# Sums of weights made ahead in DRAM, and 43 units of seven half products in place of 26

## What is computed

```
def sqrelu_mlp(hn, w1, w2):                 # w1 1024 x 4096
    u = jnp.square(jax.nn.relu(hn @ w1))
    return u @ w2

def swiglu(h, w_in, w_out):                 # w_in 1024 x 5632, run twice
    gate, up = jnp.split(h @ w_in, 2, axis=-1)
    return (jax.nn.silu(gate) * up) @ w_out
```

## Time and profile before

| | |
|---|---|
| median of 3 runs | 2059.39 us (2058.56 to 2064.13) |
| the profiled execution | 2055.45 us, its span 2053.5 us |
| PE busy | 1970.8 us (96%) |
| DVE, ACT, POOL busy | 1226.9 us (60%), 806.8 us (39%), 432.2 us (21%) |
| DMA | 175.06 MB, mean 85 GB/s |

### The profile page before, as it was taken

The page is one execution under the profiler, slowest core; times in us unless marked ns, Lnnn a source line. Parts: engine busy times, 40 slices in busy tenths (PEclk is TensorE's granted clock), DMA queues, the critical chain, the costliest instruction groups (busy, mean ns, idle before and its releaser), DMA issues.

```text
span 2053.5 us, 29329 instructions
## 1 busy us (share of the span) xinstructions
PE 1970.8 (96%) x11954; PEld 1717.1 (84%) x11954; DVE 1226.9 (60%) x1633; ACT 806.8 (39%) x1069; POOL 432.2 (21%) x312
## 2 busy tenths in 40 slices
PE   8999989999999999999999999999997899999996
PEld 6788766788888888999899999998884578888895
DVE  6668756656565654122566566556897557566565
ACT  4448734533232433223353232234434444233232
POOL 2012230202113220013222121212245122032122
PEclk9999999999999998999999999999998999999998
DMA  4223111123232221211123233223131022223231
GB/s 176 103 83 115 62 62 62 62 103 103 86 103 100 91 95 42 82 42 42 62 83 103 83 103 104 83 103 103 62 106 40 22 83 102 103 83 103 99 106 62
DMA packets 27850, 175.06 MB, mean 85 GB/s; under 512 B 4409, under 2 KB 4537, under 8 KB 7762
## 3 DMA queue, kind: packets, MB, share of 16 engines
q1 hardware_dynamic: 25680, 167.32, 23.6%
q0 software_dynamic: 1888, 5.90, 0.9%
q10 hardware_dynamic: 162, 0.10, 0.0%
HBM read 171.19 MB, written 4.78 MB: 86 GB/s over the span
## 4 chain that ended last, share of the span: by engine, by line
PE 72%; issue 12%; DVE 6%; POOL 4%; ACT 4%; DMA 2%; SPq 0%; POOLq 0%; DVEq 0%; ACTq 0%
PE lin L533 50%; PE lin L1833 6%; PE aux L1833 5%; POOL squares L752 2%; DMA w_raw<-in_weights 1%; PE aux L1425 1%; ACT w_hi L442 1%; PE aux L2645 1%; PE lin L1627 1%; PE lin L1380 1%; DVE w_lo L449 1%; PE lin L2615 1%; POOL w_lo L449 1%; PE aux L2629 1%; POOL r_t L2245 1%
## 5 line engine op out<-in xcount | busy, mean ns | idle before, releaser
L533 PE MATMUL lin<-x_hi,w_hi 128*128 128x512 f32 (+1 forms) x1160 | 408.8, 352 | 14.5 <-DVE tmp L628 6.5
L533 PE MATMUL lin<-x_hi,w_lo 128*128 128x512 f32 (+1 forms) x1160 | 407.0, 351 | 0.0
L533 PE MATMUL lin<-x_lo,w_hi 128*128 128x512 f32 (+1 forms) x1160 | 406.8, 351 | 0.0
L449 DVE TENSOR_TENSOR w_lo<-w_raw,w_hi 128x2048 fp32r<-128x2048 f32 (+1 forms) x118 | 276.3, 2341 | 176.4 <-ACT w_hi L442 175.6
L533 PE MATMUL lin<-v_hi,w_hi 128*128 128x264 f32 (+1 forms) x1088 | 365.3, 336 | 9.0 <-DVE tmp L1873 4.1
L533 PE MATMUL lin<-v_hi,w_lo 128*128 128x264 f32 (+1 forms) x1088 | 361.3, 332 | 0.0
L533 PE MATMUL lin<-v_lo,w_hi 128*128 128x264 f32 (+1 forms) x1088 | 360.9, 332 | 0.0
L442 ACT ACTIVATE w_hi<-w_raw 128x2048 fp32r<-128x2048 f32 (+1 forms) x129 | 242.8, 1882 | 206.2 <-PE lin L533 196.1
L533 PEld LDWEIGHTS lin<-x_hi,w_hi 128*128 128x128 f32 x1160 | 219.4, 189 | 49.5 <-DVE tmp L628 7.3
L533 PEld LDWEIGHTS lin<-x_hi,w_lo 128*128 128x128 f32 x1160 | 219.7, 189 | 29.9
L533 PEld LDWEIGHTS lin<-x_lo,w_hi 128*128 128x128 f32 x1160 | 219.5, 189 | 30.0 <-issue 0.2
(11 more groups left out here) (449 smaller groups left out, 3937.7 us busy)
## 6 DMA issues: line engine op xcount, KB each, us to landing
w_raw<-in_weights SPq DMA_DIRECT2D x155, 1024.0 KB, 4.8
rel_by_distance<-rel_by_distance POOLq DMA_DIRECT2D x1, 2599.5 KB, 20.3
rel_bias<-rel_by_distance POOLq DMA_DIRECT2D x8, 264.0 KB, 3.0
h<-in_x_t SPq DMA_DIRECT2D x4, 512.0 KB, 7.7
out_t<-h SPq DMA_DIRECT2D x4, 512.0 KB, 2.8
o_t<-in_mem_t POOLq DMA_DIRECT2D x1, 1024.0 KB, 4.9
cst<-in_consts SPq DMA_DIRECT2D x1, 512.0 KB, 9.3
col<-in_cols ACTq DMA_DIRECT2D x1, 67.0 KB, 5.5
```

The costliest lines, as they stand in the source:

```text
L449: does.tensor_tensor(w_lo[:, s, 0:n], w_raw[:, s, 0:n], w_hi[:, s, 0:n].bitcast(F32), ALU.subtract).then_inc(sem("w_lo_ready"), 1)
L533: last = nc.tensor.matmul(o, a, b, start=(k % (L.kc // k_banks) == 0 and p == 0), stop=((k + 1) % (L.kc // k_banks) == 0 and p == 2))
```

## The change

Four things are changed.

1. **More quad units**: (1, 2, 3) of ff1b to ff1d, (3 to 7), (1 to 7), (1 to 5) of up0a to up0c and of up1a to up1c. That is 9 + 17 + 17 = 43, of which 34 follow a quad unit directly.
2. **The sums are made in DRAM.** A new tensor `weight_sums` has 1 MB for each quad unit. POOL issues, for each of three groups (ff1, up0, up1), DMAs that copy the units there (`pool_quad_base`), add block 0 and block 1 to blocks of the copy by accumulating DMAs (`pool_quad_pairs`), then add sums to blocks of the copy (`pool_quad_triples`, 256 KB for each unit, and `pool_quad_fours`, as much). Signs and the order of blocks in a packed unit are changed so that additions do, and DVE and ACT code follows. SP now loads for a quad unit three DMAs: 768 KB of the unit, 256 KB of a sum in place of the fourth block, and 768 KB of sums into `w_sum`; its loop is written out.
3. **`ws_lo` without DVE.** ACT writes `ws_hi` = rounded `w_sum`, then `ws_lo` = minus the rounded `w_sum`; then POOL issues an accumulating DMA that adds `weight_sums` to `ws_lo` (768 KB read from DRAM). Both have two buffers. PE waits for that DMA (`quad_ws_lo0`, `quad_ws_lo1`) before p6. DVE's last part of the split, and the release of `w_lo_ready`, is now block 0, in the SwiGLU layers after the second row of the quad unit that runs.
4. PSUM releases and ACT's order are adapted to quad units side by side, and the memory set aside for descriptors goes from its default to 4096 bytes of a partition.

```
-QUADS = {"ff1b": (1, 3), "ff1c": (1, 3), "ff1d": (1, 3),
-         **{f"up{n}{part}": at for n in range(2) for part, at in zip("abc", ((3, 5, 7), (1, 3, 5, 7), (1, 3, 5)))}}
+QUADS = {"ff1b": (1, 2, 3), "ff1c": (1, 2, 3), "ff1d": (1, 2, 3),
+         **{f"up{n}{part}": at for n in range(2)
+            for part, at in zip("abc", ((3, 4, 5, 6, 7), (1, 2, 3, 4, 5, 6, 7), (1, 2, 3, 4, 5)))}}
...
+        def pool_quad_base(pool, group, *parts):
+            for run in SUM_RUNS[group]:
+                if run[0][3] in parts:
+                    pool.dma_start(quad_rows(run, w_sums, 0, 4), quad_rows(run, weights, 0, 4))\
+                        .then_inc(sem("sum_base"), 16)
+
+        def pool_quad_pairs(pool, group):
+            pool.wait_ge(sem("sum_base"), sums_made(group))
+            for run in SUM_RUNS[group]:
+                pool.dma_start(quad_rows(run, w_sums, 3, 4), quad_rows(run, weights, 0, 1), accum_op=ALU.add)\
+                    .then_inc(sem("sum_pair"), 16)
+                pool.dma_start(quad_rows(run, w_sums, 0, 1), quad_rows(run, weights, 1, 2), accum_op=ALU.add)\
+                    .then_inc(sem("sum_pair"), 16)
...
+        def pool_quad_fours(pool, group):
+            pool.wait_ge(sem("sum_s2"), sums_made(group))
...
+                pool.dma_start(quad_rows(run, w_sums, 2, 3), quad_rows(run, w_sums, 1, 2), accum_op=ALU.add)\
+                    .then_inc(sem("sum_s4"), 16)
+
+        def pool_quad_lows(pool, *names):
...
+                    pool.wait_ge(sem("quad_minus"), q + 1)
+                    pool.dma_start(ws_lo[:, q % 2, :], w_sums[q][:, 0:3 * BLOCK_W], accum_op=ALU.add)\
+                        .then_inc(sem(f"quad_ws_lo{q % 2}"), 16)
+
+        def sp_unit(sp, unit):
...
+            sp.dma_start(w_raw[:, s, BLOCK_W:], weights[unit][:, BLOCK_W:]).then_inc(sem(f"w_loaded{s}"), 16)
+            sp.wait_ge(sem("sum_pair"), 2 * made)
+            sp.dma_start(w_raw[:, s, 0:BLOCK_W], w_sums[q][:, 3 * BLOCK_W:]).then_inc(sem(f"quad_s1_{s}"), 16)
+            if q:
+                sp.wait_ge(sem("quad_minus"), q)
+            sp.wait_ge(sem("sum_s4"), made)
+            sp.dma_start(w_sum[:, :], w_sums[q][:, 0:3 * BLOCK_W]).then_inc(sem("quad_sums"), 16)
...
-                act.wait_ge(sem("quad_sum"), 4 * q + 4)
-                nc.scalar.activation(ws_hi[:, :], w_sum[:, :], ACT.Copy).then_inc(sem("w_hi_ready"), 1)
+                act.wait_ge(sem("quad_sums"), 16 * (q + 1))
+                nc.scalar.activation(ws_hi[:, q % 2, :], w_sum[:, :], ACT.Copy).then_inc(sem("w_hi_ready"), 1)
+                nc.scalar.activation(ws_lo[:, q % 2, :], w_sum[:, :], ACT.Copy, scale=-1.0).then_inc(sem("quad_minus"), 1)
...
                 if name == "p6":
+                    pe.wait_ge(sem(f"quad_ws_lo{q % 2}"), 16 * (q // 2 + 1))
                     pe.wait_ge(sem("quad_lo"), N.quads0 + 4)
...
+            pool_quad_fours(pool, "up0")
             pool_gates(pool)
             pool_squares(pool, l_ffn0, l_ffn0.idx)
-            pool_quad_sums(pool, "up0a", "up0b", "up0c")
+            pool_quad_base(pool, "up1", *"abc")
+            pool_quad_lows(pool, "up0a", "up0b", "up0c")
             pool_squares(pool, l_mix1, l_mix1.idx)
+            pool_quad_pairs(pool, "up1")
...
             dve_splits(pool, AQ, nc.gpsimd)
+            pool_quad_triples(pool, "up1")
             pool_latent_lo(pool)
             for L in (DK, DV):
                 dve_splits(pool, L, nc.gpsimd)
+            pool_quad_fours(pool, "up1")
             pool_attend(pool)
...
-    nc = bacc.Bacc("TRN2", target_bir_lowering=False, num_devices=1)
+    nc = bacc.Bacc("TRN2", target_bir_lowering=False, num_devices=1, dynamic_dma_scratch_size=4096)
```

More of the change, by code:

```diff
@@ L352, in build, with runs_of @@
         quad_seq = {u: q for q, u in enumerate(quad_units)}
+        quad_layer = {L.unit0 + u: L.name for L in layer.values() for u in L.quads}
+        def runs_of(at):
+            if len({b - a for a, b in zip(at, at[1:])}) < 2:
+                return [at]
+            cuts = [0] + [x + 1 for x in range(len(at) - 1) if at[x + 1] > at[x] + 1] + [len(at)]
+            return [at[a:b] for a, b in zip(cuts, cuts[1:])]
+        SUM_RUNS = {group: [(name, run) for name in QUADS if name[0:3] == group for run in runs_of(QUADS[name])]
+                    for group in ("ff1", "up0", "up1")}
@@ L372, in pool_quad_sums, with quad_rows @@
-        def pool_quad_sums(pool, *names):
-            for name in names:
-                for t in layer[name].quads:
-                    for step in range(4):
-                        quad_sum(pool, layer[name].unit0 + t, step)
+        def quad_rows(run, t, a, b):
+            units = [layer[run[0]].unit0 + u for u in run[1]]
+            if t is w_sums:
+                t = t[quad_seq[units[0]]:quad_seq[units[-1]] + 1]
+            else:
+                t = t[units[0]:units[-1] + 1:units[1] - units[0] if len(units) > 1 else 1]
+            return t[:, :, a * BLOCK_W:b * BLOCK_W].rearrange("q p n -> p q n")
@@ new lines, in sums_made @@
+        def sums_made(group):
+            return 16 * sum(len(SUM_RUNS[g]) for g in list(SUM_RUNS)[0:list(SUM_RUNS).index(group) + 1])
+        def pool_quad_base(pool, group, *parts):
[10 more added lines that the diff above has]
+                    .then_inc(sem("sum_pair"), 16)
@@ L400, in quad_lo @@
             if part == 3:
[L401 to L403 removed]
                 return
[L405 removed]
+            a, b = ((1, 2), (2, 4), (0, 1))[part]
             dve.wait_ge(sem("quad_w_hi"), 3 * q + part + 1)
[L407 to L409 removed]
+            low = nc.vector.tensor_tensor(w_block(w_lo, unit, a, b), w_block(w_raw, unit, a, b),
+                                          w_block(w_hi, unit, a, b).bitcast(F32), ALU.subtract)
+            if part == 2:
+                low.then_inc(sem("w_lo_ready"), 1)
         def for_units(eng, L, body, peel=False):
@@ L2886, in _ @@
             sp.dma_start(h[:, :, 0:META], meta_t).then_inc(sem("meta_loaded"), 16)
-            with sp.Fori(1, n_units // 2) as i:
-                for s in range(2):
-                    sp.wait_ge(sem("w_lo_ready"), 2 * i + s - 1)
-                    sp.dma_start(w_raw[:, s, :], one_unit(2 * i + s)).then_inc(sem(f"w_loaded{s}"), 16)
-            if n_units % 2:
-                sp.wait_ge(sem("w_lo_ready"), n_units - 2)
-                sp.dma_start(w_raw[:, 0, :], weights[n_units - 1]).then_inc(sem("w_loaded0"), 16)
+            for unit in range(2, n_units):
+                sp_unit(sp, unit)
             for t in range(0, KD, 2):
```

131 lines of the change are left out of this document (80 added, 51 removed).

## The result

The changed kernel takes 2312.76 us (median of 4 runs, 2309.98 to 2320.46), the kernel before beside it 2061.76 (2058.56 to 2065.43): a ratio of 1.122, interval 1.120 to 1.125, or 251 us more. The forecast was 2100 and its range ended at 2150. The profiled execution took 2320.46 us, its span is 2318.7, and the mean granted clock is 0.929 where it was 0.981.

What follows compares the result with a forecast made beforehand. PE was taken to bound the MLPs, every matmul saved being time saved if weights and sums are ready. The terms summed to +40.4 on the profiled 2055.45; with 3.9 for the median, 2100 us; range 2037 to 2150.

Steps and rivals of the forecast that it cites:

- Term 1: MLPs: seventeen common units become quad units, each 1.49 or 1.22 us shorter on PE; -22.6 us.
- term 5: Up layers: the last `w_lo` block behind the second row delays 28 units by 0.1 us each; +3 us (0 to 6).
- Term 2: Start of up0a: PE waits for `ws_lo` queued behind copies of up1's 17 units; +26 us (9 to 40).
- the second of the two bounds: Copies of up1's units: at 355 GB/s they take 50 us, or 69 beside the weight loads.
- the slow ends: First `ws_lo` of up0a: copies take 69 us and `ws_lo` lands 6 later, giving a wait of 40.
- the faster bound: Copies of up1's units: at the pace of loads they take 42 us, or 58 beside the weight loads.
- Term 3: Additions ahead of other POOL work: bias loads in the attention +15 us (9 to 20), `c_lo` +1, gates +1.
- Term 4: Quad units side by side: `ws_lo` 0.8 us late at every second of 34 units; +14 us (0 to 35).
- The prediction's own high bound: The `ws_lo` DMA: read from both sides and beside the load of `w_sum`, its 768 KB take 8.0 us.
- if each p6 waits several us ... the time passes 2150: Sign in the quad units: such waits would mean that the accumulating DMA is slower than twice a load.
- The clock: Behind the gap at the start of up0a: PE at half speed; +3 us (0 to 5).
- B: Rival: DRAM to DRAM copies go at the trace copy's pace, 136 us instead of 58; 2178 us; chance 0.12.

Runs made afterwards that it cites:

- e3: e2 with `ws_lo` made by one DVE subtraction, without the negated copy and the DMA into `ws_lo`; sums still not made: 2049.57 us, ratio 0.993.
- e7: e3 with the last block of the next `w_lo` ahead of the sum of three products in up0 and up1: 2029.82 us, ratio 0.984.
- e4: The changed kernel with up1's copies issued behind the DMAs of up0's `ws_lo` instead of ahead of them: 2299.97 us, ratio 1.114.
- e1: The changed kernel with 9216 instead of 4096 bytes for DMA descriptors: 2220.1 us, ratio 1.075.
- e2: The changed kernel without making the sums in DRAM; readers take packed weights, the accumulating DMA for `ws_lo` stays: 2157.7 us, ratio 1.045.
- e8: The changed kernel with `ws_lo` made by one DVE subtraction again; sums in DRAM and their place stay: 2144.9 us, ratio 1.040.
- v1: e8 with the sums of up0 and up1 issued earlier, where POOL isn't wanted for 290 us and more: 2062.76 us, ratio 1.000.
- v3: v2 with up1's copies, pairs and triples issued behind the first mixer's squares instead of beside up0: 2043.35 us, ratio 0.991.
- v2: v1 with the last block of the next `w_lo` ahead of the sum of three products in up0 and up1: 2056.64 us, ratio 0.997.

## Why the prediction was wrong, step by step

**What bounds the kernel.** Right: PE on the path in the MLPs, and the danger in DMAs on POOL's queue.

**Term 1, the gain of the quad units.** Right in kind. Side by side and undisturbed they take 10.19 us, as the earlier trace rows say. With term 5 the prediction had -19.6; e3 measured -14, and e7, in which the w_lo step is out of the way, -34. The -34 isn't all matmuls: in the two traces with nearly the same granted clock (0.981 before, 0.980 in e7) PE's busy time fell by 23.8 us, close to the 22.6, and the rest is a higher clock in the other executions of e7 (0.981 to 0.984; before beside it 0.977 to 0.982).

**Term 2, the copies ahead of `ws_lo`.** Right in place and mechanism, 36.4 us in place of 26, within its 9 to 40. The copies do run at 357 GB/s, with the loads beside them, the second of the two bounds, and `ws_lo` landed 73.6 us after their issue, near the 75 that the slow ends gave (69 and 6). The value was taken from the faster bound. That transfers of one queue go one behind the other was an assumption; this wait agrees with it, and so does e4, where the first wait fell from 36.4 to 6.8 us.

**Term 3, additions ahead of other work.** This is the step that failed in its mechanism. Every issue was counted at 0.56 us, and `c_lo` and the gates at 1 us each; they came 21.5 and 22.4 late, and the bias 28 instead of 15. Two more such places, the squares behind up0's pairs (37.5) and a split behind up1's pairs (11.9), weren't in the sum at all. The prediction asked how long the transfers take and who waits for their results; it didn't ask whether POOL can issue them. The diff had a hint, 4096 bytes set aside for descriptors; the prediction doesn't price it. What the default would have given wasn't run. The rate of an addition was well bounded ("at most twice"): 171 against 357 GB/s. The bias was mis-sized all the same, because the doubled price was that of a lone load, 2.5 us a MB: at 171 GB/s its 4.25 MB take 26 us, an estimate, and the wait is there in e1 too, without any stop.

**Term 4, `ws_lo` of units side by side.** This is the term that failed most in its size. The pattern, every second unit, was near in the up layers (20 waits in e2 at 34 quad units); in ff1 8 of 9 quad units waited. Two waits of over 7 us stood at the first quad units of up0a and up1a, behind a common unit, which the 34 of the sum leave out. The landing was put between 4.2 and 8.0 us and measured 9.7 to 9.8; a wait was not 0.8 us but 77.8 / 28 = 2.8 on average, so 78 in place of 14, and 35 as the high end was far too low. The prediction's own high bound had a load beside it and counted the addition as two reads, an estimate of its author, but all at a lone load's pace. Its sign "if each p6 waits several us ... the time passes 2150" came true; of the reason that it gave, an addition slower than twice a load, this much holds: 9.8 is 2.3 times the 4.2 of a lone load, but 1.6 times the 6.3 of the plain copy beside the same load.

**The clock.** Counted at 3 us, behind one gap. The half speed is in the trace of before: windows of 2 us from 1550 to 1558 read 0.50 each. The size failed too: in e2, with no wait for `ws_lo` over 7.5 us, 77.8 us of such waits came with 41 us more of PE's busy time than in e3. In the profiled execution of the changed kernel the span grew by 265 us: 228 of waits and 37 of busy time. The same matmuls took 1961.7 us in e3, so the quad units gave 9 back and the lower clock took 46. Long waits can do less of this: e8 has 81 us more of PE's waits than e3 on four lines with one long wait each, and PE's busy time is 1962.9 against 1961.7. It isn't a rule: e1, which lacks four long waits of the changed kernel, has 16.7 us less of busy time than it (1991.1).

**Term 5, `w_lo_ready`.** Foreseen at 3 us (0 to 6), for the right 28 units; 0.28 a unit by the trace's waits (0.36 in the unit shown) instead of 0.1 made 8 to 10.

**The chances.** The forecast's high end added high ends of terms that were there. None of the rivals was a stop of POOL inside an issue. The waits that it made, 37.5 + 21.5 + 22.4 + 11.9 = 93 us where the sum had 2, are nearly what e1 won back. B, copies at 131 GB/s, came nearest in time, for a reason that didn't hold (the copies moved 357).

## What to carry to other kernels

Before moving work from an engine to DMAs of a queue, ask three things of each: can the issuing engine get rid of it, what stands behind it on the engine and on the queue, and is its landing shorter than the time between issue and use, at an accumulation's rate. Bulk transfers that nobody needs soon belong where the issuing engine is idle for longer than they take and the loads beside them want little; v1 and v3 won 82 and 13 us by place alone (from e8, and from v2). A low part that DVE makes in 1.75 us (e3) shouldn't be traded for a landing of 9.8 (e2), even when DVE is the busier engine.
